# Gates of the second expert table loaded for eight blocks at once; activations to another place

## The chip, the cores and the metric

One core of one Trainium2 chip runs the kernel. The metric is device time in microseconds (us); 3909.4 us is the median of three runs of the kernel before (3905.04 to 3912.0). TensorE (PE in the profile) multiplies, with its weight loads shown apart as PEld. VectorE is DVE, ScalarE is ACT, GpSimd is POOL and SyncE is SP. Sixteen DMA engines move the data of all queues.

## The reference

One decoder layer for 512 tokens of width 2048, in float32. Only the last part matters for this change: a channel mixer that chooses, for each token and each of 8 heads, 16 out of 16384 one-neuron experts.

```
expert, gate = top-16 of the product keys, softmax of their scores
act = gelu(x . u_tab[expert])                    # per token, head, slot
y   = sum over heads and slots of gate * act * v_tab[expert]
h   = LN(alpha * h + y)
```

## The kernel before

The 512 tokens are two halves of 256. The first half takes its experts by gather: POOL fetches rows of 8 KB per partition (1 MB for 128 tokens), first of `peer_u`, then of `peer_v`, and DVE multiplies each with the tokens (L1184, L1189). The second half treats the experts densely: all 16384 activations for 256 tokens are computed by matrix products with the whole first table (64 units, the U stage), and the result is multiplied with the whole second table (64 units of 2 MB of weights, the V stage). The gathers of the first half run beside both stages, one or two rows per V unit (403 of the 512 rows come before the last of the planned phases, the rest in V).

Between U and V stand two scratch tensors in DRAM. `act_spill` holds the gelu of U, in 32 groups of four blocks of 128 experts. `gate_spill` holds the gates, scattered to dense form by one-hot products, in 8 chunks of 32 tokens: for each chunk and each partition all 128 blocks, 32 tokens each. A group's gates are thus 8 pieces per partition, each of 4 x 32 floats = 512 bytes, 512 KB in all. A group's activations are 4 KB per partition, also 512 KB.

In V each group q serves two units. SP loads it by `load_e(q)` (L439 for the activations, L440 for the gates); DVE multiplies the two (`e_mult`, L1615); ACT rounds the product (`move_e`, L619); DVE forms the remainder (`e_rest`, L1621), which frees the buffers of that parity, and `load_e(q + 2)` waits for that. `e_mult(q)` stands some three units behind the issue of `load_e(q)`.

The weights of a unit come in two loads of 1 MB (c = 0 and 1, `load`, L401 and L402), into two buffers used in turn. Load c = 0 of unit n waits until half of unit n - 2 is used, load c = 1 until unit n - 2 is done. Each quarter of a unit is rounded by ACT (`split_hi`, L554) into a single buffer `w_hi`, then DVE writes the remainder over the weights (`split_lo`, L1235), then PE has 12 matmuls for it (L1151). So a quarter's rounding waits for the weights and for the quarter that leaves `w_hi`, and DVE runs its gathered rows between the remainders in an order written out by hand.

SP is one in-order queue. In V its order is: both loads of an even unit, `load_e`, both loads of the odd unit. The loop body holds two such groups. Before V, `load_e(0)` and `load_e(1)` go out together eight units before the end of U, and `load_e(2)` between the first two units of weights of V. The buffers: `e_act` and `e_gate` share the place of `aT`, 8 KB per parity; the one-hots lie where the sub-keys were (`skT`), and are no longer used once the gates are in DRAM.

Of the kernel before, what the change touches and what calls it, by code (L numbers as in the profile page):

```python
# [14 lines left out]
F32 = mybir.dt.float32  # L15
F32R = mybir.dt.float32r
U32 = mybir.dt.uint32
ALU = mybir.AluOpType
# [3 lines left out]
P = 128  # L22
D = 2048
SEQ = 512
HALF = 256
# [32 lines left out]
N_V = N_U + U_UNITS  # L58
GROUPS = 32
GCHUNK = 32  # L60
# [67 lines left out]
def build(nc, x, w_units, b_gate, sinks, conv_w, ln1_g, ln1_b, peer_sub_keys, peer_u, peer_v, ln2_g, ln2_b, out):  # L128
    ctx = ExitStack()
    with ctx:  # L130
# [3 lines left out]
        def over(tensor_at, name, shape, dt=F32R):  # L134

            return nc.alloc_sbuf_tensor_at(name, shape, dt, offset=tensor_at)

        def at(name, shape):

            t = sb(name, shape)  # L140
            return t, nc.sbuf_base - 4 * shape[1] * (shape[2] if len(shape) > 2 else 1)

        def sem(name):
            return ctx.enter_context(nc.semaphore(name))
# [7 lines left out]
        aT, aT_at = at("aT", [P, KT, HALF])  # L152
# [9 lines left out]
        skT, skT_at = at("skT", [P, 2 * PH, NK])  # L162
# [41 lines left out]
        gbuf = [over(at_, f"gbuf{i}", [P, NK, GCHUNK], F32) for i, at_ in enumerate((aT_at, mT_at))]  # L204
        e_hi = [over(mT_at + 8192 * i, f"e_hi{i}", [P, 4, HALF]) for i in range(2)]
        e_lo = [over(mT_at + 8192 * i + 4096, f"e_lo{i}", [P, 4, HALF]) for i in range(2)]
        e_act = [over(aT_at + 8192 * i, f"e_act{i}", [P, 4, HALF], F32) for i in range(2)]
        e_gate = [over(aT_at + 8192 * i + 4096, f"e_gate{i}", [P, HALF // GCHUNK, 4, GCHUNK], F32) for i in range(2)]
        one_hot = [over(skT_at + 4096 * i, f"one_hot{i}", [P, 2, 4, NK], F32) for i in range(2)]

        act_spill = nc.dram_tensor("act_spill", (GROUPS, P, 4 * HALF), F32, kind="Internal").ap()
        gate_spill = nc.dram_tensor("gate_spill", (HALF // GCHUNK, P, GROUPS, 4 * GCHUNK), F32, kind="Internal").ap()

        def by_k(n):

# [147 lines left out]
        gate_sent = sem("gate_sent")  # L363
        act_sent = [sem(f"act_sent{i}") for i in range(4)]
        e_in = [sem(f"e_in{i}") for i in range(2)]
        e_prod = sem("e_prod")
        e_hi_ready = sem("e_hi_ready")
        e_lo_ready = sem("e_lo_ready")
# [16 lines left out]
        @block.sync  # L385
        def _(sp):
            sp.dma_start(h0[:, :, :], x_v[:, 0:TILES, :]).then_inc(x_in, 16)
            def load(n, per=0, i=0):

                for c in range(2):  # L390
                    if n >= N_V:
                        at_ = 2 * (n - N_V) + c
                        src = v_blocks[:, bass.ds((2 * per) * i + at_, 1), :].rearrange("p o d -> p (o d)")
                    else:
                        at_ = 2 * (n % UNITS if n < N_U else UNITS + n - N_U) + c
                        src = w_units[bass.ds((2 * per) * i + at_, 1), :, :].rearrange("o p x -> (o p) x")
                    if n >= 2 and c == 0:
                        sp.wait_ge(quarter_used, (3 * per) * i + (3 * (n - 2) + 2))
                    if n >= 2 and c == 1:
                        sp.wait_ge(dense_ready, per * i + (n - 1))  # L400
                    sp.sem_inc(went_on, 1)  # L401
                    sp.dma_start(wbuf[n % 2][:, 2 * c:2 * c + 2, :].rearrange("p j x -> p (j x)"), src  # L402
                                 ).then_inc(w_ready[2 * (n % 2) + c], 16)

            for b in range(HALVES):
                n0 = UNITS * b
                if b:
                    sp.wait_ge(dense_ready, U_OUT)
                    sp.dma_start(h1, x_v[:, TILES:2 * TILES, :]).then_inc(x_in, 16)
                for n in range(n0, n0 + U_Q + 1):  # L410
                    load(n)
                    if n == 0:
                        sp.dma_start(subk, peer_sub_keys.rearrange("l h a n c -> n (l h a) c")).then_inc(small_in, 16)
                        sp.dma_start(vecs_in[0:32, :], b_gate.rearrange("l (c p) -> (l c) p", p=P)).then_inc(small_in, 16)
                        sp.dma_start(vecs_in[32:80, :], conv_w.rearrange("l w (c p) -> (l w c) p", p=P)).then_inc(small_in, 16)
                        sp.dma_start(sink[:, :], sinks[0, :].partition_broadcast(P)).then_inc(small_in, 16)
                with sp.Fori(0, (U_OUT - U_Q) // 4) as i:
                    for c in range(4):
                        load(n0 + U_Q + 1 + c, 4, i)
                if b:  # L420
                    sp.wait_ge(dense_ready, n0 + U_OUT)
                    sp.dma_start(h1, x_v[:, TILES:2 * TILES, :]).then_inc(xres_in, 16)
                for n in range(n0 + U_OUT + 1, n0 + U_PQ):
                    load(n)
                sp.wait_ge(dense_ready, n0 + U_OUT)
                sp.dma_start(ln1[:, 0, :], ln1_g[0, :].partition_broadcast(P)).then_inc(ln1_in, 16)
                sp.dma_start(ln1[:, 1, :], ln1_b[0, :].partition_broadcast(P)).then_inc(ln1_in, 16)
                for n in range(n0 + U_PQ, n0 + UNITS):
                    load(n)

            def load_e(q, i=0):

                src = act_spill[q, :, :] if q < 2 else \
                    act_spill[bass.ds(2 * i + q, 1), :, :].rearrange("o p x -> (o p) x")
                gates = gate_spill[:, :, bass.ds(2 * i + q, 1), :].rearrange("c p o x -> p c (o x)")
                if q >= 2:
                    sp.wait_ge(e_lo_ready, 2 * i + (q - 1))
                sp.sem_inc(went_on, 1)
                sp.dma_start(e_act[q % 2][:, :, :].rearrange("p b t -> p (b t)"), src).then_inc(e_in[q % 2], 16)  # L439
                sp.dma_start(e_gate[q % 2][:, :, :, :].rearrange("p c b t -> p c (b t)"),  # L440
                             gates).then_inc(e_in[q % 2], 16)

            with sp.Fori(0, (U_UNITS - 8) // 2) as i:
                for c in range(2):
                    load(N_U + c, 2, i)
            sp.wait_ge(gate_sent, 16 * (HALF // GCHUNK))
            for j in range(4):
                sp.wait_ge(act_sent[j], 16)
            load_e(0)
            load_e(1)  # L450
            for j in range(U_UNITS - 8, U_UNITS):
                load(N_U + j)
            load(N_V)
            load_e(2)
            load(N_V + 1)
            sp.wait_ge(dense_ready, N_V)
            sp.dma_start(ln2[:, 0, :], ln2_g[0, :].partition_broadcast(P)).then_inc(ln2_in, 16)
            sp.dma_start(ln2[:, 1, :], ln2_b[0, :].partition_broadcast(P)).then_inc(ln2_in, 16)
            for j in range(4):
                sp.wait_ge(act_sent[j], 16 * (U_UNITS // 4))  # L460
            with sp.Fori(0, GROUPS // 2 - 2) as i:
                for g in range(2):
                    load(N_V + 2 + 2 * g, 4, i)
                    load_e(3 + g, i)
                    load(N_V + 3 + 2 * g, 4, i)
            load(N_V + U_UNITS - 6)
            load_e(GROUPS - 1)
            for m in range(U_UNITS - 5, U_UNITS):
                load(N_V + m)
# [701 lines left out]
        def _(dve):  # L1171
            V = nc.vector
# [83 lines left out]
            for b in range(HALVES):  # L1256
# [89 lines left out]
                for i in range(2):  # L1346
                    for c in range(4):
                        n = n0 + U_CONV + 12 * i + 3 * c
                        f = conv0[b] + cs * c
# [55 lines left out]
                for i in range(4):  # L1405
                    base = n0 + U_GC + 4 * i
                    for c in range(4):
# [3 lines left out]
                        if c >= 2:  # L1411
                            g = stage[(n - 2) % 4]
# [197 lines left out]

            def e_mult(q):

                dve.wait_ge(e_in[q % 2], 32 * (q // 2 + 1))
                e = e_act[q % 2][:, :, :].rearrange("p b (c t) -> p b c t", c=HALF // GCHUNK)
                V.tensor_tensor(e, e, e_gate[q % 2][:, :, :, :].rearrange("p c b t -> p b c t"), ALU.mult  # L1615
                                ).then_inc(e_prod, 1)

            def e_rest(q):
# [16 lines left out]
            for j in range(U_UNITS):  # L1635
                n = N_U + j
                if j == IDX_AT:
                    dve.wait_ge(idx_done, TILES)

                def between():  # L1640
                    g = G_PER * (j + 1 - G_FIRST)
                    if 0 <= g < HALF // 4:
                        for k in range(G_PER):
                            one_hots(g + k)
                    if n + 4 >= N_V and n % 2 == 0:
                        e_mult((n + 4 - N_V) // 2)
                    if n + 4 >= N_V and n % 2:
                        e_rest((n + 3 - N_V) // 2)

                section(n, between)  # L1650
# [16 lines left out]
            for t in range(TILES):  # L1667
                f = 12 * t
# [70 lines left out]
```

## Time and profile before

| what | value |
|---|---|
| median of three runs | 3909.4 us |
| the profiled execution: its own time / its span | 3916.73 us / 3914.9 us |
| PE busy | 3766.4 us, 96% |
| DVE busy | 2720.5 us, 69% |
| ACT busy | 1379.6 us, 35% |
| POOL busy | 1096.0 us, 28% |
| DMA moved | 1236.87 MB, 316 GB/s on the mean |

The table gives busy time of each engine as the profile's first part has it, in one execution. PE's share is a mean over stages; whether PE or something else sets the pace of a stage is read from the stage's own windows and waits. The DMA share of a stretch is the busy share of the 16 DMA engines; it can read slightly over 1, since packets overlap at their ends.

### The profile page before, as it was taken

What the parts mean: (1) busy time and instruction counts of PE and PEld (TensorE: products, weight loads), DVE (VectorE), ACT (ScalarE), POOL (GpSimd) and SP (SyncE); (2) the same over time, 40 slices, a digit from 0 to 9 for tenths busy, and PEclk for the clock granted to TensorE, in tenths of its full rate; (3) what the DMA queues carried; (4) which work ended last, traced back from release to release, by engine and by line L of the source; (5) the groups of instructions that cost most, each with busy time, mean ns of one, the idle gap of its engine ahead of it and who ended that gap; (6) DMA issues with size and microseconds to landing.
All of it is one profiled execution on the core that took longest, in us unless ns stands there. A gap on an engine that the chain in (4) does not pass through costs nothing.

```text
span 3914.9 us, 60806 instructions
## 1 busy us (share of the span) xinstructions
PE 3766.4 (96%) x24471; PEld 3482.9 (89%) x24471; DVE 2720.5 (69%) x3355; ACT 1379.6 (35%) x1966; POOL 1096.0 (28%) x587
## 2 busy tenths in 40 slices
PE   8999999998999999999999889999998888999997
PEld 8999999998988888888888889999998877878785
DVE  4544555455788765566655577888887887888898
ACT  5544444443323100000000334566663333344342
POOL 0000000001634444344433532211113442334442
PEclk9999999999999999999999999999999999999998
DMA  5345555554689999999999449999999999999996
GB/s 186 109 155 182 182 182 182 184 183 169 241 346 384 409 421 399 405 391 408 394 393 391 169 144 354 364 374 376 360 360 396 409 409 376 409 400 393 393 410 243
DMA packets 209849, 1236.87 MB, mean 316 GB/s; under 512 B 20176, under 2 KB 53536, under 8 KB 66336
## 3 DMA queue, kind: packets, MB, share of 16 engines
q1 hardware_dynamic: 124448, 659.65, 44.3%
q0 software_dynamic: 73728, 536.90, 33.6%
q10 hardware_dynamic: 11520, 38.28, 2.4%
q8 instruction: 95, 1.56, 0.2%
q14 instruction: 58, 0.48, 0.0%
HBM read 1196.48 MB, written 37.75 MB: 315 GB/s over the span
## 4 chain that ended last, share of the span: by engine, by line
PE 82%; DMA 9%; DVE 7%; issue 1%; ACT 1%; SPq 0%; ACTq 0%; DVEq 0%
PE dense_ps L909 23%; PE dense_ps L898 13%; PE dense_ps L899 13%; PE dense_ps L900 13%; PE dense_ps L1151 6%; DMA wbuf<-in_peer_v_dram 4%; PE dense_ps L939 3%; PE score_ps L1151 3%; DMA row<-in_peer_v_dram,expert 3%; DVE h L1189 3%; DMA wbuf<-in_w_units_dram 2%; PE o_ps L1151 1%; PE oT_ps L1151 1%; PE score_ps L1108 1%; PE o_ps L1032 1%
## 5 line engine op out<-in xcount | busy, mean ns | idle before, releaser
L1235 DVE TENSOR_TENSOR w_lo<-wbuf,w_hi_r 128x1024 fp32r<-128x1024 f32 x808 | 982.3, 1222 | 575.5 <-ACT w_hi_r L554 575.0
L554 ACT ACTIVATE w_hi_r<-wbuf 128x1024 fp32r<-128x1024 f32 x872 | 915.4, 1059 | 1155.5 <-PE dense_ps L900 631.1
L898 PE MATMUL dense_ps<-act_hi,w_hi_r 128*128 128x256 f32 x4128 | 1185.3, 287 | 49.1 <-DVE w_lo L1235 42.2
L899 PE MATMUL dense_ps<-act_lo,w_hi_r 128*128 128x256 f32 x4128 | 1174.9, 285 | 0.0
L900 PE MATMUL dense_ps<-act_hi,w_lo 128*128 128x256 f32 x4128 | 1174.8, 285 | 0.0
L898 PEld LDWEIGHTS dense_ps<-act_hi,w_hi_r 128*128 128x128 f32 x4128 | 798.9, 194 | 59.8 <-DVE w_lo L1235 34.0
L505 POOL DMA_INDIRECT row<-in_peer_v_dram,expert x256 | 494.6, 1932 | 1127.5 <-DVE h L1189 1103.2
L899 PEld LDWEIGHTS dense_ps<-act_lo,w_hi_r 128*128 128x128 f32 x4128 | 799.0, 194 | 0.0
L900 PEld LDWEIGHTS dense_ps<-act_hi,w_lo 128*128 128x128 f32 x4128 | 798.4, 193 | 0.0
L909 PE MATMUL dense_ps<-xT,wbuf 128*128 128x256 f32 x3136 | 688.1, 380 | 0.8 <-ACT xT L539 0.8
L909 PEld LDWEIGHTS dense_ps<-xT,wbuf 128*128 128x128 f32 x3136 | 594.3, 190 | 86.2 <-issue 5.3
L1189 DVE SCALAR_TENSOR_TENSOR h<-row,dots,h 128x2048 f32<-128x2048 f32 x256 | 600.9, 2347 | 27.8 <-DMA row<-in_peer_v_dram,expert 27.5
L505 POOL DMA_INDIRECT row<-in_peer_u_dram,expert x256 | 443.4, 1732 | 613.4 <-DVE row L1184 553.4
L1184 DVE SCALAR_TENSOR_TENSOR row<-row,h 128x2048 f32<-128x2048 f32 x256 | 572.6, 2287 | 27.6 <-DMA row<-in_peer_u_dram,expert 27.5
L496 POOL TENSOR_TENSOR w_lo<-wbuf,w_hi_r 128x1024 fp32r<-128x1024 f32 x64 | 155.2, 2435 | 1022.4 <-ACT w_hi_r L554 1022.4
L1151 PE MATMUL dense_ps<-w_hi_r,e_hi 128*128 128x512 f32 x512 | 162.7, 399 | 32.4 <-DVE w_lo L1235 31.7
L1151 PE MATMUL dense_ps<-w_lo,e_hi 128*128 128x512 f32 x512 | 159.2, 392 | 0.0
L1151 PE MATMUL dense_ps<-w_hi_r,e_lo 128*128 128x512 f32 x512 | 159.1, 392 | 0.0
L766 ACT ACTIVATE stage<-dense_ps 128x512 f32<-128x512 f32 x48 | 28.7, 598 | 361.7 <-PE dense_ps L909 317.2
L1151 PEld LDWEIGHTS dense_ps<-w_hi_r,e_hi 128*128 128x128 f32 x512 | 95.0, 190 | 61.0 <-DVE w_lo L1235 40.0
L898 PE MATMUL dense_ps<-br_hi,w_hi_r 128*128 128x256 f32 x512 | 145.0, 283 | 1.0 <-ACT br_hi L718 1.0
L900 PE MATMUL dense_ps<-br_hi,w_lo 128*128 128x256 f32 x512 | 144.9, 283 | 0.0
(220 smaller groups left out, 4214.2 us busy)
## 6 DMA issues: line engine op xcount, KB each, us to landing
wbuf<-in_w_units_dram SPq DMA_DIRECT2D x456, 1024.0 KB
wbuf<-in_peer_v_dram SPq DMA_DIRECT2D x128, 1024.0 KB
act_spill<-stage ACTq DMA_DIRECT2D x64, 256.0 KB, 8.8
gate_spill<-gbuf ACTq DMA_DIRECT2D x8, 2048.0 KB, 11.2
e_act<-act_spill SPq DMA_DIRECT2D x32, 512.0 KB, 10.7
e_gate<-gate_spill SPq DMA_DIRECT2D x32, 512.0 KB, 13.1
cT<-in_x_dram SPq DMA_DIRECT2D x2, 2048.0 KB, 11.3
row<-in_peer_u_dram,expert POOLq DMA_INDIRECT x256
```

Of the source, the lines that this page charges most:

```text
L496: nc.gpsimd.tensor_tensor(w_lo[n % 2][:, j, :], wbuf[n % 2][:, j, :], w_hi[:, j, :].bitcast(F32), ALU.subtract).then_inc(lo_by_pool, 1)
L505: pool.indirect_dma_start(out=row[SLOT[g]][:, :], out_offset=None, in_=(u_tab if g < U_ROWS else v_tab)[:, :], in_offset=bass.IndirectOffs ...
L554: act.activation(w_hi[:, j, :], wbuf[n % 2][:, j, :], ACT.Copy).then_inc(w_hi_ready, 1)
L898: nc.tensor.matmul(out, w[0], x[0], start=opens, stop=False)
L899: nc.tensor.matmul(out, w[0], x[1], start=False, stop=False)
L900: return nc.tensor.matmul(out, w[1], x[0], start=False, stop=closes)
L909: last = nc.tensor.matmul(dense_ps[n % 4][:, c, :], w_part(wbuf[n % 2], n, k, j), src[:, k, :], start=opens and k == 0, stop=closes and k ...
L939: last = nc.tensor.matmul(dense_ps[n % 4][:, t, :], src[:, k, tok], w_part(wbuf[n % 2], n, k, j), start=t == 0 and k == 0, stop=t == TILES ...
L1151: last = nc.tensor.matmul(ffn_ps[t][j % 2 * 2 + c], e[:, blk, tok], w[:, j, c * 512:(c + 1) * 512], start=opens and j < 2 and at == 0, sto ...
L1184: V.scalar_tensor_tensor(out=row[slot][:, :], in0=row[slot][:, :], scalar=1.0, in1=h0[:, t, :], op0=ALU.mult, op1=ALU.mult, accum_out=dots ...
L1189: V.scalar_tensor_tensor(out=h0[:, t, :], in0=row[slot][:, :], scalar=dots[:, t, col:col + 1], in1=h0[:, t, :], op0=ALU.mult, op1=ALU.add) ...
L1235: V.tensor_tensor(w_lo[n % 2][:, j, :], wbuf[n % 2][:, j, :], w_hi[:, j, :].bitcast(F32), ALU.subtract).then_inc(lo_by_dve, 1)
```

## The change

The gates of two groups are loaded by one DMA, in pieces of 8 x 32 floats = 1 KB, 1 MB in all, with the even group; the odd group loads only its activations. The gates get semaphores of their own. `e_gate` now takes all 16 KB of `aT`, and `e_act` moves to the place of the one-hots. The layout of `gate_spill` in memory is the same as before, as another view. SP's loop body holds four groups in place of two.

```diff
-        e_act = [over(aT_at + 8192 * i, f"e_act{i}", [P, 4, HALF], F32) for i in range(2)]
-        e_gate = [over(aT_at + 8192 * i + 4096, f"e_gate{i}", [P, HALF // GCHUNK, 4, GCHUNK], F32) for i in range(2)]
+        e_act = [over(skT_at + 4096 * i, f"e_act{i}", [P, 4, HALF], F32) for i in range(2)]
+        e_gate = [over(aT_at + 8192 * i, f"e_gate{i}", [P, HALF // GCHUNK, 8, GCHUNK], F32) for i in range(2)]
...
-        gate_spill = nc.dram_tensor("gate_spill", (HALF // GCHUNK, P, GROUPS, 4 * GCHUNK), F32, kind="Internal").ap()
+        gate_spill = nc.dram_tensor("gate_spill", (HALF // GCHUNK, P, GROUPS // 2, 8 * GCHUNK), F32, kind="Internal").ap()
...
+        gates_in = [sem(f"gates_in{i}") for i in range(2)]
...
             def load_e(q, i=0):
 
-                src = act_spill[q, :, :] if q < 2 else \
-                    act_spill[bass.ds(2 * i + q, 1), :, :].rearrange("o p x -> (o p) x")
-                gates = gate_spill[:, :, bass.ds(2 * i + q, 1), :].rearrange("c p o x -> p c (o x)")
                 if q >= 2:
-                    sp.wait_ge(e_lo_ready, 2 * i + (q - 1))
+                    sp.wait_ge(e_lo_ready, 4 * i + (q - 1))
                 sp.sem_inc(went_on, 1)
-                sp.dma_start(e_act[q % 2][:, :, :].rearrange("p b t -> p (b t)"), src).then_inc(e_in[q % 2], 16)
-                sp.dma_start(e_gate[q % 2][:, :, :, :].rearrange("p c b t -> p c (b t)"),
-                             gates).then_inc(e_in[q % 2], 16)
+                sp.dma_start(e_act[q % 2][:, :, :].rearrange("p b t -> p (b t)"),
+                             act_spill[bass.ds(4 * i + q, 1), :, :].rearrange("o p x -> (o p) x")).then_inc(e_in[q % 2], 16)
+                if q % 2 == 0:
+                    gates = gate_spill[:, :, bass.ds(2 * i + q // 2, 1), :].rearrange("c p o x -> p c (o x)")
+                    sp.dma_start(e_gate[q // 2 % 2][:, :, :, :].rearrange("p c b t -> p c (b t)"),
+                                 gates).then_inc(gates_in[q // 2 % 2], 16)
...
-            with sp.Fori(0, GROUPS // 2 - 2) as i:
-                for g in range(2):
-                    load(N_V + 2 + 2 * g, 4, i)
+            with sp.Fori(0, GROUPS // 4 - 1) as i:
+                for g in range(4):
+                    load(N_V + 2 + 2 * g, 8, i)
                     load_e(3 + g, i)
-                    load(N_V + 3 + 2 * g, 4, i)
+                    load(N_V + 3 + 2 * g, 8, i)
...
-                dve.wait_ge(e_in[q % 2], 32 * (q // 2 + 1))
+                dve.wait_ge(e_in[q % 2], 16 * (q // 2 + 1))
+                dve.wait_ge(gates_in[q // 2 % 2], 16 * (q // 4 + 1))
                 e = e_act[q % 2][:, :, :].rearrange("p b (c t) -> p b c t", c=HALF // GCHUNK)
-                V.tensor_tensor(e, e, e_gate[q % 2][:, :, :, :].rearrange("p c b t -> p b c t"), ALU.mult
+                gates = e_gate[q // 2 % 2][:, :, 4 * (q % 2):4 * (q % 2) + 4, :].rearrange("p c b t -> p b c t")
+                V.tensor_tensor(e, e, gates, ALU.mult
                                 ).then_inc(e_prod, 1)
```

## Rows read from the trace of the kernel before

**Rows 1.** The page: busy time of PE; DMA busy in tenths over 40 slices
```profile
PE 3766.4 (96%) x24471; PEld 3482.9 (89%) x24471; DVE 2720.5 (69%) x3355; ACT 1379.6 (35%) x1966; POOL 1096.0 (28%) x587
...
DMA  5345555554689999999999449999999999999996
```

**Rows 2.** Windows: stretch, length, busy PE PEld DVE ACT POOL, clock, DMA share, GB/s
```profile
3146.00:3888.00 742.00, 710.29 (x3068) 579.48 (x3069) 641.60 (x450) 292.53 (x287) 280.82 (x115) 0.98 0.98 388
...
1900.00:2100.00 200.00, 195.41 (x896) 171.36 (x895) 104.37 (x102) 12.96 (x22) 78.04 (x43) 0.98 0.97 399
```

**Rows 3.** Chain of waits from 3160 on, its weight loads: start us, us, what
```profile
3168.81 18.30 DMA wbuf<-in_peer_v_dram
...
3218.21 23.20 DMA wbuf<-in_peer_v_dram
...
3273.91 14.37 DMA wbuf<-in_peer_v_dram
...
3319.41 13.48 DMA wbuf<-in_peer_v_dram
...
3407.52 14.16 DMA wbuf<-in_peer_v_dram
...
3499.12 18.33 DMA wbuf<-in_peer_v_dram
...
3637.21 16.64 DMA wbuf<-in_peer_v_dram
...
3706.04 13.85 DMA wbuf<-in_peer_v_dram
...
3816.12 14.89 DMA wbuf<-in_peer_v_dram
```

**Rows 4.** Timeline of SP's queue around one group: start us, us, instruction, count
```profile
3728.33 17.56 SPq L402 DMA_DIRECT2D wbuf<-in_peer_v_dram  x4
3746.15 0.33 SPq L439 DMA_DIRECT2D e_act<-act_spill  x1
3746.67 0.38 SPq L440 DMA_DIRECT2D e_gate<-gate_spill  x1
3751.00 16.68 SPq L402 DMA_DIRECT2D wbuf<-in_peer_v_dram  x4
```

**Rows 5.** Timeline of ACT, same group: the wait before it and its releaser last
```profile
3763.99 2.01 ACT L554 ACTIVATE w_hi_r<-wbuf 128x1024 fp32r<-128x1024 f32 x2 [5.76 <-DMA wbuf<-in_peer_v_dram]
```

**Rows 6.** Windows of 20 us around one late load, columns as rows 2
```profile
3500.00:3520.00 20.00, 15.29 (x69) 12.34 (x67) 11.53 (x9) 5.65 (x6) 2.62 (x2) 0.96 1.03 413
3520.00:3540.00 20.00, 20.00 (x78) 16.27 (x79) 20.00 (x14) 9.21 (x9) 10.18 (x4) 0.87 0.95 359
```

**Rows 7.** DMA queues, 1900 to 2100: packets, MB, share of 16 engines
```profile
q1 hardware_dynamic: 4312, 31.52, 37.8%
```

**Rows 8.** DMA packets and queues, 3164 to 3812
```profile
DMA packets 64481, 257.59 MB, mean 398 GB/s; under 512 B 4369, under 2 KB 33041, under 8 KB 36625
...
q1 hardware_dynamic: 49466, 148.20, 59.1%
q0 software_dynamic: 14860, 108.24, 41.4%
```

**Rows 9.** DMA packets and SP's queue, 3019 to 3022, gates of groups 0 and 1
```profile
DMA packets 1124, 1.02 MB, mean 341 GB/s; under 512 B 43, under 2 KB 1001, under 8 KB 1117
...
q1 hardware_dynamic: 1102, 0.97, 101.7%
```

**Rows 10.** Tile e_gate: ns min/median/max, first to last start; time to landing
```profile
L1615 DVE TENSOR_TENSOR e_act<-e_act,e_gate x32: 1212/1220/1229, 3116.6 to 3843.5; 128x1024 f32<-128x1024 f32 x32
...
DMA to landing us min/median/max: 6.0/13.1/24.9
```

**Rows 11.** Timeline of SP's queue, second load of the first pair
```profile
3006.79 8.25 SPq L439 DMA_DIRECT2D e_act<-act_spill  x1
3015.09 2.08 SPq L440 DMA_DIRECT2D e_gate<-gate_spill  x1
```

## The prediction

> **What bounds the kernel now.** I read the page first. PE is busy 96% of the span, so most of the kernel is PE's; but the DMA slices stand at 9 from about 1.3 ms on, except for a short dip, and to the end [rows 1]. The change touches only the last quarter, so I next took windows of it. In the V stage, 3146 to 3888, PE is busy 710.3 of 742 us, and its clock is 0.98 of full. The DMA engines are busy 0.98 of that same stage, at 388 GB/s [rows 2]. Two resources are close to full. What decides between them is the chain of waits. From 3160 on it goes through PE's matmuls, and is broken nine times by a weight load that took 13.5 to 23.2 us from issue to landing [rows 3]. Every one of the nine is the first load of an odd unit, the one that stands right behind `load_e` in SP's queue. In one such group SP issues the last load of the even unit before 3745.9, the activations at 3746.15, the gates at 3746.67, and the odd unit's first load at 3751.00 [rows 4]. ACT can round it only at 3763.99, after 5.76 us of waiting: it took 13.0 us to land [rows 5]. That one was in time for PE. The one issued at 3499.12 took 18.33 us, and PE lost 4.71 us in the 20 us window around it [rows 3, 6]. So a load is in time if it lands within about 18.33 - 4.71 = 13.6 us. Applied to all nine, the excess over 13.6 is 4.7 + 9.6 + 0.8 + 0 + 0.6 + 4.7 + 3.0 + 0.3 + 1.3 = 25.0 us, of the 31.7 us in which PE is idle in V. The V stage is therefore PE's, with holes cut by DMA queues that are full.
>
> **What the gate loads cost now.** From 3164 to 3812 there are 33041 - 4369 = 28672 packets of 512 bytes to 2 KB, which is 28 groups of 1024 pieces [rows 8]. SP's queue took 0.591 x 648 x 16 = 6127 us of engine time for 148.20 MB, 41.3 us per MB; the gathers' queue took 0.414 x 648 x 16 = 4292 for 108.24 MB, 39.7. Earlier, with no small pieces in it, SP's queue took 0.378 x 200 x 16 / 31.52 = 38.4 us per MB [rows 7]. The excess over the two is (41.3 - 39.7) x 148.2 = 237 and (41.3 - 38.4) x 148.2 = 430 us, which over 28672 pieces is 8 and 15 ns each. A third reading is a stretch in which almost nothing but SP's queue moved: 48.8 us of engine time for 0.97 MB with 958 such pieces. At 39.7 us per MB the bytes account for 38.5, and the other 10.3 are 11 ns per piece [rows 9]. I take 11: it stands between the two and is the most direct.
>
> What the rows show is 341 GB/s in that stretch of small pieces against 399 over a stretch of large ones [rows 2, 9]. The Trainium skill's page "DMA: Bandwidth & Descriptors", section Specifications, has 512 bytes as the least size for full rate; by that rule the pieces are already large enough, the change would save nothing, and the time would be that of the second rival. The same page, section "Why small descriptors are slow (HBM only)", gives a fixed cost per packet as well; that direction agrees with the trace.
>
> **The change, part by part.**
> 1. Half as many pieces. 32 x 1024 become 16 x 1024. 16384 x 11 ns / 16 engines = 11.3 us less DMA time, 0.35 us per group of two units. Bounds: 8 and 15 ns give 8 and 15 us. The trace has no 1 KB piece in it: if their own excess were gone too, it would be twice 11.3, 23 us; if they cost double, nothing. I take a fixed cost per piece.
> 2. What stands ahead of the weights. The even group's SP order now has 1.5 MB between the even and the odd unit's weights, the odd group's 0.5 MB, against 1 MB in each. SP's queue moves 1.05 x 3 MB from about 3745.8 to 3764.0, 173 GB/s beside the gathers [rows 4, 5]. So 0.52 MB is 3.0 us. The even group's number of small packets stays 1024, so only the bytes are added there, and I take + 2.6 us; the odd group loses 3.0.
>  Now the nine late loads. Counting `load_e` along SP's queue, they follow groups 3, 5, 7, 9, 13, 17, 23, 26 and 31: eight of nine are odd and gain 3.0 us. Their excess becomes 1.7 + 6.6 + 0 + 0 + 0 + 1.7 + 0 + 0 = 10.0 us instead of 24.7. The even one (3706.04) rises from 0.3 to 2.9. Of the even groups that are in time now, the one of rows 4 goes from 13.0 to 15.6, 2.0 us late; the others land at 12 us or less, and I put 1.5 us on them together. Sum 10.0 + 2.9 + 2.0 + 1.5 = 16.4 instead of 25.0: 8.6 us less. This static sum and the 11.3 us of part 1 are two readings of one gain and are not added. Where DMA alone paced the stage it would be 11.3; I take 8.6, since PE has a stage of its own to reach.
> 3. The pair ahead of V. SP stood 8.25 + 2.08 us in issuing the second pair of loads [rows 11], with weights of U behind it. Then 2 MB go before them as now, in 1024 fewer pieces (0.7 us, in the 11.3 already), and one issue less. The first gate load fills the queue with as many pieces as before, of twice the bytes, so its stall may be up to 10 us too; the weights behind it wait for the same 2 MB either way. I count 0, with - 2 to + 2 as bounds. `load_e(2)` puts 0.52 MB more ahead of the second unit of V: + 3 us on a load there, of which the gathered rows on which that part of the chain waits hide most: 0 to + 2 in the range, 0 taken.
> 4. The new wait of DVE. `e_mult` waits for activations and gates apart. The last `load_e` is issued just ahead of 3816.12 and the last multiplication is at 3843.5; the median gate load lands after 13.1 us, the latest after 24.9 [rows 3, 10]. Twice the bytes adds 3 us. In the median case some 15 us remain; behind that wait stand DVE's remainders, and PE behind them, if it ever were late. For odd groups the gates are there a group earlier. Nothing counted; one late load of the 24.9 kind would cost 1 to 3 us.
> 5. The rest costs nothing: the same 32 multiplications of 1220 ns, on the same number of elements [rows 10], other addresses for the activations, 16 DMA issues of 0.38 us less on SP [rows 4], which waits for PE anyway, and the longer loop body.
>
> Sum: - 8.6 us on the profiled execution, 3916.7 to 3908. Its time is 7.3 us above the median of the runs, so against 3909.4 it is **3901 us**, 0.22% less.
>
> **The rivals.**
> - *The burst wins.* Place: the odd unit's weights behind an even group's 1.5 MB. That eight of nine late loads are odd now may be no more than that an idle spell of PE lets DMA catch up for the following group; an odd group with less to load no longer gives an even one that relief. Then the even groups have the latencies of the odd ones (the eight in the chain have 16.7 us on the mean [rows 3]; with the other seven taken at 12 it is 14.5) plus 2.6, so 3.5 us late each in 15 groups, 52 us, and odd ones nothing: 52 - 25 = + 27, less the 11 us of part 1, + 16: 3925 us. It decides from the point at which even loads land later than 13.6 us in most groups. Against it: the gathers are ahead after an odd group, and leave the queue to the burst.
> - *No change.* The freed DMA time goes to idle DMA engines: after the late load of 3499 the DMA share falls from 1.03 to 0.95 and PE's clock is 0.87 in the next window [rows 6]. If larger swings make that 1 us in 11 of the 15 even groups, the 11 us are gone: 3909. It would also come so if 1 KB pieces cost double, or if the excess of SP's queue came from something other than its small pieces.
> - *More than counted.* No excess at 1 KB (part 1, 23 us) would end most of the holes: 25.0 us of late loads and part of the clock loss (0.02 x 742 = 15 us). With 23 us less DMA time, of which two thirds reach PE, - 15: 3894.
>
> **How the numbers follow.** Forecast 0.42 (3896 to 3906), more than counted 0.13, no change 0.24, burst 0.21. A measurement of this kernel tells 0.2%, 7.8 us, from no change. The forecast lies just beyond that and falls on both sides of it, some 0.30 and 0.12. Faster: 0.30 + 0.13 + 0.03 of the others = 0.46. Slower, from the burst above all: 0.19. The same: 0.35. The range runs from the larger gain to short of the full burst: 3890 to 3919.
>
> **What would show it.** The page should have 16384 packets fewer under 2 KB, and SP's queue 11 x 16 = 176 us less engine time, 0.3% of its share. In the V stage SP's queue should be near 40 us per MB. PE's idle time in V should fall from 31.7 to about 23 us, with late loads in the chain behind even groups now; if it grows and they all stand behind even groups, the burst won. The prediction is wrong in its size if the stage's DMA rate doesn't rise above 398 GB/s [rows 8], and in its mechanism if DVE waits for gates or if the time moves outside of the last 900 us.

## The result, and the profile after

The changed kernel is slower: 3934.7 us on the median of five runs (3918.6 to 3945.6) against 3909.4. The ratio is 1.0055, with a 95% interval of 1.0037 to 1.0073. Forecast were 3901 us and a range to 3919. Later, beside other kernels, it gave 1.0055 again (3930.5 us).

The profiled execution is the longest of the five, 3945.6 us, so its losses are some 11 us larger than those of the median. What stands here is the page of that execution: PE's busy time and the DMA slices, as in [rows 1], and the packets.

```profile
PE 3776.3 (96%) x24471; PEld 3489.2 (88%) x24471; DVE 2721.6 (69%) x3355; ACT 1382.0 (35%) x1966; POOL 1098.2 (28%) x587
...
DMA  5345555554699999999999449999999999899996
...
DMA packets 193209, 1236.87 MB, mean 314 GB/s; under 512 B 19920, under 2 KB 36896, under 8 KB 49696
```

Half of the gates' pieces are gone: 53536 packets under 2 KB became 36896, and the bytes are the same. PE has 9.9 us more busy time for the same number of matmuls, and near the end stands an 8 in the DMA slices where there were only nines. The V stage from its first matmul to its last ones, before and in the changed kernel (columns as [rows 2], whose window of before is 0.5 us shorter):

```profile
3145.90:3888.40 742.50, 710.74 (x3070) 579.86 (x3071) 642.10 (x450) 292.53 (x287) 280.82 (x115) 0.98 0.98 388
3138.70:3917.00 778.30, 725.93 (x3070) 590.75 (x3071) 642.59 (x450) 294.30 (x287) 280.86 (x115) 0.96 0.93 369
```

The stage took 778.3 us, before 742.5. PE was idle 52.4 of them instead of 31.8; its clock was 0.96 instead of 0.98, and its busy time grew by 15.2 us. The DMA share fell from 0.98 to 0.93 and the rate from 388 to 369 GB/s: the DMA engines stood still for longer. So 35.8 us more in V are 20.6 us of waiting and 15.2 us of slower matmuls. The start of V came 7 us earlier.

Both of these executions are above the median of their kernel, by 11 and by 7 us. Two that are close to it are those of experiment 1 (all of the change but the joined load, 3904.0 us) and of experiment 10 (the changed kernel again, 3929.2 us). They give the same picture in a smaller size: 26.4 us more in V, of which 14.2 are idle time of PE and 12.2 slower matmuls.

```profile
3139.70:3875.30 735.60, 708.39 (x3070) 580.15 (x3071) 641.58 (x450) 293.32 (x287) 289.21 (x115) 0.98 0.99 391
3138.50:3900.50 762.00, 720.60 (x3070) 585.27 (x3071) 642.49 (x450) 293.85 (x287) 283.89 (x115) 0.97 0.95 378
```

The chain of waits of the changed kernel, its weight loads in V (start us, us, what), the counterpart of [rows 3]:

```profile
3149.95 18.06 DMA wbuf<-in_peer_v_dram
3209.30 13.71 DMA wbuf<-in_peer_v_dram
3231.49 18.17 DMA wbuf<-in_peer_v_dram
3282.33 14.14 DMA wbuf<-in_peer_v_dram
3327.58 20.86 DMA wbuf<-in_peer_v_dram
3381.22 18.27 DMA wbuf<-in_peer_v_dram
3433.21 18.17 DMA wbuf<-in_peer_v_dram
3575.44 20.70 DMA wbuf<-in_peer_v_dram
3628.03 13.55 DMA wbuf<-in_peer_v_dram
3672.69 18.58 DMA wbuf<-in_peer_v_dram
3723.34 15.77 DMA wbuf<-in_peer_v_dram
3770.93 17.22 DMA wbuf<-in_peer_v_dram
3821.23 15.96 DMA wbuf<-in_peer_v_dram
```

From 3231 on all eleven stand behind the 1.5 MB of an even group, groups 6 to 30 (16 and 18 are not in the chain). Their mean is 17.4 us. The second, of 3209.30, stands behind group 5; the first stands behind no group but behind the 2 MB of `ln` that SP loads at the start of V. Over 13.6 us all thirteen sum up to 46 us, and PE was idle 52. The late load of 3327.58 shows what one costs. First SP's queue around it (start us, us), then ACT and POOL, with the wait before each and its releaser, then windows of 5 us (columns as [rows 2]):

```profile
3322.73 0.33 SPq L437 DMA_DIRECT2D e_act<-act_spill  x1
3323.26 0.38 SPq L441 DMA_DIRECT2D e_gate<-gate_spill  x1
3327.58 16.69 SPq L403 DMA_DIRECT2D wbuf<-in_peer_v_dram  x4
```

```profile
3348.53 2.00 ACT L555 ACTIVATE w_hi_r<-wbuf 128x1024 fp32r<-128x1024 f32 x2 [13.71 <-DMA wbuf<-in_peer_v_dram]
```

```profile
3356.78 3.95 POOL L506 DMA_INDIRECT row<-in_peer_v_dram,expert  x1 [17.43 <-DVE h L1190]
```

```profile
3342.00:3347.00 5.00, 1.65 (x8) 1.03 (x6) 0.00 (x0) 0.00 (x0) 0.00 (x0) 0.92 1.01 426
3347.00:3352.00 5.00, 1.10 (x3) 0.92 (x4) 2.38 (x3) 2.98 (x4) 0.00 (x0) 0.50 1.02 428
3352.00:3357.00 5.00, 5.00 (x14) 3.95 (x13) 5.00 (x4) 1.60 (x3) 0.22 (x1) 0.56 0.60 238
3357.00:3362.00 5.00, 5.00 (x24) 4.13 (x23) 4.58 (x5) 1.58 (x3) 3.73 (x1) 1.00 0.26 77
```

One stall can be followed through all queues. The odd unit's weights are issued at 3327.58 and land at 3348.5, 20.9 us later. ACT waits 13.7 us for them, so DVE, whose next instruction is a remainder of those weights, does nothing from 3342 to 3347, although a gathered row lies ready for it (one issued at 3317.27 had landed at 3331.2): it stands behind the remainder in DVE's order. POOL gets no row buffer back for 17.4 us and issues nothing. The DMA engines finish what is queued, at 426 and 428 GB/s, and then run dry: 0.60 and 0.26 busy, 238 and 77 GB/s. PE comes back at a clock of 0.50 and 0.56, that is mostly at 1.2 GHz instead of 2.4, after having been idle for 7.3 of the 10 us from 3342 to 3352. A stall of 7 us is thus paid twice on PE: its idle time, and its slow matmuls after it. The DMA time that lies idle is no third term of V's 35.8 us; that it is missing later, and makes further loads late, is my reading, and no run tests it.

### The profile page after: what moved, and what is told of

Read it like the earlier page. It is cut to its first block, busy times and chain, and to the rows that moved or that the text cites. A ratio compares the mean times of both kernels' runs of the same rounds, so it can differ in the third digit from the quotient of the medians.

```text
span 3943.6 us, 60773 instructions
## 1 busy us (share of the span) xinstructions
PE 3776.3 (96%) x24471; PEld 3489.2 (88%) x24471; DVE 2721.6 (69%) x3355; ACT 1382.0 (35%) x1966; POOL 1098.2 (28%) x587
## 2 busy tenths in 40 slices
DMA packets 193209, 1236.87 MB, mean 314 GB/s; under 512 B 19920, under 2 KB 36896, under 8 KB 49696
## 4 chain that ended last, share of the span: by engine, by line
PE 82%; DMA 10%; DVE 6%; issue 1%; ACT 1%; SPq 0%; ACTq 0%; DVEq 0%
PE dense_ps L910 23%; PE dense_ps L899 13%; PE dense_ps L900 13%; PE dense_ps L901 13%; DMA wbuf<-in_peer_v_dram 6%; PE dense_ps L1152 6%; PE dense_ps L940 3%; PE score_ps L1152 3%; DMA row<-in_peer_v_dram,expert 3%; DVE h L1190 2%; PE score_ps L1109 2%; PE o_ps L1033 1%; PE o_ps L1152 1%; PE oT_ps L1152 1%; DMA wbuf<-in_w_units_dram 1%
```

## The experiments

All are timed against the kernel before, which ran beside them. Ratios have their 95% interval. For the V stage the windows of the profiled executions are read.

**1. All of the change but the joined load.**

```diff
-                if q % 2 == 0:
-                    gates = gate_spill[:, :, bass.ds(2 * i + q // 2, 1), :].rearrange("c p o x -> p c (o x)")
-                    sp.dma_start(e_gate[q // 2 % 2][:, :, :, :].rearrange("p c b t -> p c (b t)"),
-                                 gates).then_inc(gates_in[q // 2 % 2], 16)
+                h = q % 2
+                gates = gate_spill[:, :, bass.ds(2 * i + q // 2, 1), 128 * h:128 * h + 128].rearrange("c p o x -> p c (o x)")
+                sp.dma_start(e_gate[q // 2 % 2][:, :, 4 * h:4 * h + 4, :].rearrange("p c b t -> p c (b t)"),
+                             gates).then_inc(gates_in[h], 16)
...
-                dve.wait_ge(gates_in[q // 2 % 2], 16 * (q // 4 + 1))
+                dve.wait_ge(gates_in[q % 2], 16 * (q // 2 + 1))
```

> All of the change but the joined load: e_act at the one-hots' place, e_gate in 8-block buffers with semaphores of its own, SP's loop body of four groups, but each group loads its own half of the gates, 512 KB in 512-byte pieces, as before. Burst theory (the 1.5 MB ahead of the odd unit's weights after an even group is the loss): same as before, 3909 within 5 us, PE idle in V near 32 us, late loads behind odd and even groups. Rival (places, semaphores or the longer loop body are the loss): near the changed kernel, 3925 to 3945.

3905.7 us, 0.9996 (0.9983 to 1.0008): no difference. The places, the semaphores and the longer loop body cost nothing that shows. The loss is in the joined load. One part of what I expected did not come: the late loads do not stand behind odd and even groups. All six weight loads in this kernel's chain stand behind odd ones (groups 3, 5, 13, 17, 21 and 23), as eight of nine did before:

```profile
3161.55 18.17 DMA wbuf<-in_peer_v_dram
3210.87 22.34 DMA wbuf<-in_peer_v_dram
3396.08 14.40 DMA wbuf<-in_peer_v_dram
3489.51 14.55 DMA wbuf<-in_peer_v_dram
3578.73 14.17 DMA wbuf<-in_peer_v_dram
3624.04 18.43 DMA wbuf<-in_peer_v_dram
```

So with the old order of loads the pattern by parity comes again, in another kernel and another execution.

**2. 1 KB pieces, but 0.5 MB of gates with each group.**

```diff
+                def gates(p, c0, c1):
+                    sp.dma_start(e_gate[p % 2][:, c0:c1, :, :].rearrange("p c b t -> p c (b t)"),
+                                 gate_spill[c0:c1, :, bass.ds(2 * i + p, 1), :].rearrange("c p o x -> p c (o x)")
+                                 ).then_inc(gates_in[p % 2], 16)
                 if q % 2 == 0:
-                    gates = gate_spill[:, :, bass.ds(2 * i + q // 2, 1), :].rearrange("c p o x -> p c (o x)")
-                    sp.dma_start(e_gate[q // 2 % 2][:, :, :, :].rearrange("p c b t -> p c (b t)"),
-                                 gates).then_inc(gates_in[q // 2 % 2], 16)
+                    gates(q // 2, 0, 4)
+                if q == 0:
+                    gates(0, 4, 8)
+                if q % 2 and q < GROUPS - 1:
+                    gates((q + 1) // 2, 4, 8)
...
-                dve.wait_ge(gates_in[q // 2 % 2], 16 * (q // 4 + 1))
+                dve.wait_ge(gates_in[q // 2 % 2], 32 * (q // 4 + 1))
```

> The changed kernel with its 1 KB pieces, but the 1 MB of a pair's gates is loaded in two halves by chunks of tokens: chunks 4 to 7 with the odd group ahead, chunks 0 to 3 with the even one. Every group again puts 1 MB ahead of the odd unit's weights. Burst theory: the loss is gone and the saving of half the pieces remains, 3898 to 3909, DMA engines not idle in V. Rival (1 KB pieces save nothing or the places cost): 3909, or 3925 and more.

3902.4 us, 0.9981 (0.9968 to 0.9994). The loss is gone. The gain over experiment 1, 0.0015, points the way that I had forecast, but the two intervals overlap. The packets and SP's queue over the V stage, first of experiment 1 (735.6 us), then of this kernel (730.9 us):

```profile
q1 hardware_dynamic: 52733, 164.20, 57.5%
```

```profile
q1 hardware_dynamic: 37392, 164.00, 56.0%
```

0.575 x 735.6 x 16 / 164.20 = 41.2 us of engine time per MB, and 0.560 x 730.9 x 16 / 164.00 = 39.9. The difference over 164 MB, some 210 us, on 15341 fewer packets is 14 ns per piece. The same sum from experiments 11 and 12 gives 12 ns. I had taken 11, with 8 and 15 as bounds.

**3. The burst in 512-byte pieces.** The gates of both groups come with the even group as in the changed kernel, by two DMAs of 512 KB in the old pieces.

```diff
                 if q % 2 == 0:
-                    gates = gate_spill[:, :, bass.ds(2 * i + q // 2, 1), :].rearrange("c p o x -> p c (o x)")
-                    sp.dma_start(e_gate[q // 2 % 2][:, :, :, :].rearrange("p c b t -> p c (b t)"),
-                                 gates).then_inc(gates_in[q // 2 % 2], 16)
+                    for h in range(2):
+                        gates = gate_spill[:, :, bass.ds(2 * i + q // 2, 1), 128 * h:128 * h + 128].rearrange("c p o x -> p c (o x)")
+                        sp.dma_start(e_gate[q // 2 % 2][:, :, 4 * h:4 * h + 4, :].rearrange("p c b t -> p c (b t)"),
+                                     gates).then_inc(gates_in[q // 2 % 2], 16)
...
-                dve.wait_ge(gates_in[q // 2 % 2], 16 * (q // 4 + 1))
+                dve.wait_ge(gates_in[q // 2 % 2], 32 * (q // 4 + 1))
```

> The changed kernel's burst, in 512-byte pieces: the gates of two groups are both loaded with the even group, by two DMAs of 512 KB. Burst theory with pieces worth 11 ns each: slower than the changed kernel by 5 to 12 us, 3935 to 3950. If the pieces are worth nothing: equal to it, about 3930.

3947.6 us, 1.0092 (1.0076 to 1.0107), above the changed kernel's 1.0055 by 0.0037, 14 us. So the burst costs with either piece, and the 1 KB pieces give back a part of it; the difference is a little over the 5 to 12 us expected. It is not the pieces' time on the DMA engines alone. In this kernel SP itself stands at the second of the two gate loads, ahead of the odd unit's weights, and the chain goes through that eleven times, 73 us in all, as here:

```profile
3331.74 7.65 SPq L442
```

The changed kernel's gate load holds SP for 0.83 us at most.

**4. Pieces of 4 KB.** As experiment 2, with 4 KB per partition taken from the activations in the gates' place.

```diff
-                if q % 2 == 0:
-                    gates = gate_spill[:, :, bass.ds(2 * i + q // 2, 1), :].rearrange("c p o x -> p c (o x)")
-                    sp.dma_start(e_gate[q // 2 % 2][:, :, :, :].rearrange("p c b t -> p c (b t)"),
-                                 gates).then_inc(gates_in[q // 2 % 2], 16)
+                p = (q + 1) // 2
+                if q < GROUPS - 1:
+                    for c0 in ((0, 4) if q == 0 else (4 * (q % 2),)):
+                        sp.dma_start(e_gate[p % 2][:, c0:c0 + 4, :, :].rearrange("p c b t -> p (c b t)"),
+                                     act_spill[bass.ds(4 * i + q, 1), :, :].rearrange("o p x -> (o p) x")
+                                     ).then_inc(gates_in[p % 2], 16)
...
-                dve.wait_ge(gates_in[q // 2 % 2], 16 * (q // 4 + 1))
+                dve.wait_ge(gates_in[q // 2 % 2], 32 * (q // 4 + 1))
```

> As even_1k in amounts and order, but what is loaded in the gates' place is one piece of 4 KB per partition and DMA, taken from the activations: the product is not the gated one, only the time is read. It takes the cost of the small pieces to nothing. If small pieces cost 11 ns each, 32768 of them take 22 us of DMA time: 3888 to 3903. If they cost nothing that reaches PE: 3905 to 3912, equal to even_1k.

3894.9 us, 0.9952 (0.9937 to 0.9967), within the range expected of costly pieces. Of the gain over the kernel before, 0.0048, 1 KB pieces gave 0.0019. But this run reads other memory as well: it loads the group's activations a second time instead of the gates. The 0.0029 between 1 and 4 KB are 11 us, while SP's queue needed only some 4 us less on each DMA engine. So it is not shown that all of the gain comes from the size of the pieces.

**5. The joined 1 MB behind the odd unit's weights.** `load_gates` holds the changed kernel's gate load; only its place in SP's order differs.

```diff
                 for g in range(4):
                     load(N_V + 2 + 2 * g, 8, i)
                     load_e(3 + g, i)
                     load(N_V + 3 + 2 * g, 8, i)
+                    load_gates(3 + g, i)
```

> The changed kernel's single DMA of 1 MB for a pair's gates, in 1 KB pieces, but issued behind both loads of the odd unit, so that it stands ahead of the next even unit's weights; 0.5 MB of activations alone stand ahead of the odd unit's. Burst theory (what counts is how much stands ahead of one load of weights; 1 MB is as before, 1.5 MB is too much): the loss is gone, 3895 to 3907. Rival (a joined 1 MB transfer is bad wherever it stands): 3920 or more.

3901.0 us, 0.9969 (0.9958 to 0.9979). The same single DMA of 1 MB, moved by one unit, costs nothing: ahead of the next weights there stands 1 MB now instead of 1.5 (the loop body above shows the move; the first three groups are loaded as in the changed kernel). What hurt was how much stood ahead of one load of weights, not that the gates came joined.

**6. 0.5 MB ahead of every unit.** The halves of experiment 2, issued where experiment 5 issues them.

> The halves of even_1k (0.5 MB of gates in 1 KB pieces per group) issued behind the odd unit's loads: 0.5 MB stands ahead of every unit's first load. Burst theory: late loads all but end, and the time is that of even_1k or less, 3885 to 3900. Rival (DMA's total work sets V's length, order does not count below 1 MB): 3902, equal to even_1k.

3889.5 us, 0.9947 (0.9933 to 0.9961): faster than both kernels of this case. Its V stage in one window:

```profile
3137.70:3860.50 722.80, 706.69 (x3070) 577.87 (x3071) 641.49 (x450) 293.10 (x287) 305.19 (x115) 0.99 0.98 397
```

PE idles 16.1 us instead of 31.8, and DMA moves 397 GB/s instead of 388. That late loads would all but end did not come: nine weight loads of 12.1 to 18.9 us are still in its chain, five of them first loads of even units, but only four are over 13.6 us.

**7. 0.75 and 0.25 MB of gates**, as experiment 2 with six and two chunks, so 1.25 and 0.75 MB ahead of the odd units' weights.

> Between even_1k and the changed kernel: six of eight chunks of a pair's gates, 0.75 MB, with the even group and 0.25 MB with the odd one, so 1.25 and 0.75 MB stand ahead of the odd units' weights. Burst theory with a threshold: about half of the changed kernel's loss or less, 3905 to 3918. If only the joined load (one large DMA) matters: 3902.

3910.3 us, 1.0007 (0.9992 to 1.0022), within the range expected: a quarter of a MB more already costs. From 1 to 1.25 MB the ratio rises by 0.0026, from 1.25 to 1.5 MB by 0.0048. That looks as if the price grew faster than the burst, but with these intervals an even growth, 1.0018 in the middle, is not excluded, and no threshold is shown.

**8 and 9. The joined load with the odd group**, twice, the second time beside the changed kernel (10).

```diff
-                if q % 2 == 0:
-                    gates = gate_spill[:, :, bass.ds(2 * i + q // 2, 1), :].rearrange("c p o x -> p c (o x)")
-                    sp.dma_start(e_gate[q // 2 % 2][:, :, :, :].rearrange("p c b t -> p c (b t)"),
-                                 gates).then_inc(gates_in[q // 2 % 2], 16)
+                p = (q + 1) // 2
+                if q == 0 or q % 2 and q < GROUPS - 1:
+                    sp.dma_start(e_gate[p % 2][:, :, :, :].rearrange("p c b t -> p c (b t)"),
+                                 gate_spill[:, :, bass.ds(2 * i + p, 1), :].rearrange("c p o x -> p c (o x)")
+                                 ).then_inc(gates_in[p % 2], 16)
```

> The changed kernel with the joined 1 MB of gates loaded one group earlier, with the odd group. My prediction's count by parity (eight of nine late loads follow odd groups, so odd groups can bear no more and even ones can): clearly slower than the changed kernel, by 15 us or more, 3945 and up. If the parity was chance, and each burst makes its own late load: equal to the changed kernel, 3925 to 3940.

3944.0 us, 1.0081 (1.0062 to 1.0101), between the two expectations. Some of its late weight loads, in the chain (start us, us):

```profile
3159.85 20.99 DMA wbuf<-in_peer_v_dram
3211.94 26.11 DMA wbuf<-in_peer_v_dram
...
3505.21 21.40 DMA wbuf<-in_peer_v_dram
...
3602.75 17.01 DMA wbuf<-in_peer_v_dram
3650.86 21.15 DMA wbuf<-in_peer_v_dram
3704.23 18.27 DMA wbuf<-in_peer_v_dram
```

Every late load behind a `load_e` in its chain follows an odd group, from 3 to 29. So the late loads go where the burst goes. That is shown by this kernel and the changed one together, since without a burst they follow odd groups too.

> The joined 1 MB with the odd group, again. The first run (3944, ratio 1.0081) lay between the two theories' numbers. If parity was chance, its interval and the changed kernel's beside it overlap, within 8 us; if odd groups really bear less, it is slower by 15 us or more.

> The changed kernel itself, beside the next three on one chip. 3920 to 3945, ratio to before 1.004 to 1.009.

3941.6 us, 1.0085 (1.0068 to 1.0103), and for the changed kernel 3930.5 us, 1.0055 (1.0038 to 1.0073). The odd burst is 11 us slower by the medians, less than the 15 us of one theory and more than the 8 us of the other, and the two intervals just overlap. Neither theory fits whole. Even groups cannot bear the burst for nothing, as my count by parity had it. Past the start of V the burst costs the same behind either parity: on the mean of groups 7 to 31 the loads behind odd groups took 16.0 and 15.5 us in experiments 8 and 9, and on the mean of groups 6 to 30 those behind even ones took 16.4 and 15.1 us in the changed kernel and experiment 10 (all from the landings in the traces). The difference sits in the first groups. Behind groups 3 and 5 the loads took 21.0 and 26.1 us in experiment 8 (21.1 and 26.6 in 9), against 18.7 and 13.7 in the changed kernel (17.3 and 13.6 in 10), which is 15 to 17 us more over the bound of 13.6. That fits the 11 us; no run moves the burst behind these two groups alone.

**11 and 12. Order against pieces.** The order of experiment 6 with 512-byte pieces (the next group's gates, 512 KB, behind each odd unit's loads), and experiment 6 again.

> The order of spread (0.5 MB of gates behind each odd unit's loads) with the old 512-byte pieces: the gates of the next group, 512 KB each. If order alone gave the gain of spread, 3890 as that; if pieces keep their worth of 7 us or so (even_1k against places_only: 3902 against 3906, ratios 0.9981 and 0.9996), 3894 to 3902; if the pieces were all of it, 3909.

> The same kernel as spread, beside its 512-byte form: 3885 to 3895, ratio to before 0.993 to 0.996.

3898.2 us, 0.9974 (0.9964 to 0.9984), and 3889.1 us, 0.9955 (0.9943 to 0.9968). By the medians the order alone, with the old pieces, gives 12 us and the 1 KB pieces give 9 more; by the ratios it is 10 and 7.

## Why the prediction was wrong

*What bounds the kernel: right.* Late weight loads behind `load_e` described the changed kernel too: 46 us over the bound of 13.6 us and 52 us of idle PE in its first profile, 29 and 41 us in that of experiment 10. The bound is a rough one: loads of 12.9 us stand in that chain too.

*Part 1, the pieces: right.* The 11 ns per piece stand between 8 and 15, and the runs give 12 to 14 (experiments 11 with 12, and 1 with 2): 12 to 14 us of DMA time instead of 11.3. What reaches the total, where the order is held fixed, is 0.0015 (experiments 1 and 2), 0.0019 (11 and 12) and 0.0037 (10 and 3), so 6, 7 and 14 us. The first is within the noise and the last has SP's own waiting in it, so 6 to 9 us is the better figure; all three have the same sign. Whether the cost is fixed per piece is open. The V stage of experiment 4 had 0.552 x 736.0 x 16 / 164.29 = 39.6 us per MB, and the kernels with 1 KB pieces and no burst 39.9 to 40.1. The 0.3 to 0.5 over 164 MB and 10693 pieces fewer are 5 to 9 ns per 1 KB piece, less than for a 512-byte piece, but the four 1 KB kernels differ by 0.2 among themselves. The Trainium skill's page "DMA: Bandwidth & Descriptors", section Specifications, has 512 bytes as enough for full rate. These runs, with the DMA engines busy 0.98 of V, do not bear it out: SP's queue took 41.0 to 41.3 us per MB with such pieces and no burst, against 39.9 to 40.1 with 1 KB.

*Part 2, the burst: this is the step that failed.* I took the nine late loads of the trace of before as given, saw that eight followed odd groups, and moved each by - 3.0 or + 2.6 us: 16.4 us of lateness in place of 25. Measured were 46, and 29 in experiment 10. The error is not that the parity was chance, for it was not. It is that the even groups' short latencies, 13.0 us and less, held only with 1 MB ahead of each group. With the burst ahead of them, ten of the thirteen loads behind groups 6 to 30 took over 13.6 us, eight of the thirteen in experiment 10. Over all fourteen even groups from 4 to 30 the mean went from 9.8 us to 15.9 (14.9 in experiment 10), by 6.1 and 5.1 us where I had added 2.6. The odd groups gained more than the 3.0 us that I took off: from 14.3 to 8.6 us (9.0) on the mean of groups 3 to 31. So with both signs the shift was about twice what I had worked out from the bytes. Why it is so much more stays open; that each late load lets DMA catch up for the next group, as the burst rival had it, fits the alternation but is not shown by a run of its own. Experiments 8 and 9 move the burst to the odd groups, and the late loads are there; experiments 2, 5 and 6 take the burst away, and the loss goes with it.

*What I had not priced.* The clock: PE's busy time for the same matmuls grew by 15.2 us in that execution. Windows of 1 us show eleven stretches of V with a lower granted clock, where the kernel before has three, and most of the stalls of PE over 2 us are followed by one. And DMA's idle time: less DMA work means less time only while the queues are never empty. The DMA engines were idle for 0.07 of 778 us instead of 0.02 of 742, some 40 us more, about three times what the pieces saved. The rival "no change" named both, but with 11 us for DMA's idle time it had them far too small.

*Parts 3 to 5: right.* Experiment 1 shows the places and the longer loop body free of cost. In the changed kernel the gates landed after 22.4 us at the latest, and DVE was never idle ahead of a multiplication by them. (The room that I gave in part 4, some 15 us, is 11 with the 3 us of twice the bytes.) V started 7 us earlier in the changed kernel's profile, beyond the 2 us that I allowed ahead of it. In all thirteen profiles of kernels with the new places it started earlier than in the one of before, by 0.5 to 12 us; as experiment 1 is no faster in all, the one profile of before doesn't settle what that is worth.

*The rivals.* The burst rival, with 0.21, was the one that came, and its place and its point of decision (even loads later than 13.6 us in most groups) were as stated. Its 3925 is between the forecast and the 3934.7 measured, and it is partly luck: it had + 27 us of lateness where + 21 came in the profiled execution, and nothing for the slower matmuls, + 15 us there. In the runs 1 KB pieces at even spacing are 0.0015 below experiment 1, and the burst adds 1.0055 - 0.9981 = 0.0074, 29 us, to them.

The signs that I had given read the same way. PE's idle time grew, and every late load from 3231 on stands behind an even group, which was the burst rival's sign. The rate in V fell to 369 GB/s instead of rising above 398. SP's queue took 0.536 x 778.3 x 16 / 164.05 = 40.7 us per MB, not quite the 40 of the forecast.

## What to carry to other kernels

When a transfer is joined with its neighbour, ask what stands behind it in the same queue, and when that is due: with both queues full, 0.5 MB more ahead of a load that is due in about 13.6 us cost 29 us, some four times the 6 to 9 us that halving the number of pieces gave. Large pieces and even spacing can be had together, by cutting the joined transfer along another axis (here chunks of tokens instead of blocks) and issuing the parts where nothing urgent follows.

In a trace in which everything waits for everything, a latency belongs to the order of loads that it was measured in. That eight of nine late loads stood behind odd groups was a fact of that order, and gave the even groups no room for more. A shift of each latency by the bytes added was only about half of what came. And a stall has to be priced with the slow matmuls behind it.

## What the runs showed of the hardware that I had not expected

After 7.3 of 10 us without matmuls PE came back at a granted clock of 0.50 and 0.56 in the two windows of 5 us in which the late load of 3327.58 had just landed and the next matmuls ran. Over V the slower matmuls added 15.2 us to its busy time.

The excess of a piece over its bytes was 12 to 14 ns at 512 bytes. At 1 KB it was some 5 to 9 ns, beside the 40 ns that its bytes take at 39.6 us per MB on one engine, by one run of 4 KB pieces.

Two gate loads of 512 KB in 512-byte pieces, one right behind the other, held SP itself for 3.9 to 10.2 us at eleven places of the chain (experiment 3). One load of 1 MB with half as many pieces held it for 0.83 us at most.
